# Sparse attention on one core: score products of two heads taken in pairs, the low-key products over 64 rows each

## The reference

```python
def dsa_attention(q, k, v, q_idx, k_idx, w_idx, k_top):
    ...
        rel = jax.nn.relu(jnp.einsum('bqhd,bsd->bqhs', qib, k_idx).astype(jnp.float32))
        score = jnp.einsum('bqhs,bqh->bqs', rel, wb.astype(jnp.float32))
        ...
        _, sel = lax.top_k(score, k_top)
        valid = sel <= qpos[None, :, None]
        kg = gather(k, sel)
        vg = gather(v, sel)
        qg = qb.reshape(bsz, Q_BLOCK, n_kv, grp, hd)
        sc = jnp.einsum('bqkgd,bqjkd->bqkgj', qg, kg).astype(jnp.float32) * scale
        sc = jnp.where(valid[:, :, None, None, :], sc, -jnp.inf)
        p = jax.nn.softmax(sc, axis=-1).astype(v.dtype)
        o = jnp.einsum('bqkgj,bqjkd->bqkgd', p, vg)
```

## Time and profile before

| | us |
|---|---|
| median of 3 runs | 3304.93 (3300.85 to 3305.95) |
| the profiled execution | 3304.05 |
| its span | 3302.3 |
| TensorE matmuls busy | 3109.3 (94%) |
| VectorE busy | 2024.6 (61%) |
| ScalarE busy | 1834.1 (56%) |
| mean granted clock of TensorE | 0.975 of full speed |

### The profile page before, as it was taken

How to read it: one execution, slowest core, us unless ns; L and a number is a source line. 1 busy time by engine, 2 the same in 40 slices (tenths; PEclk the granted TensorE clock), 3 DMA queues, 4 the chain that set the end, 5 groups by cost and what they waited for, 6 DMA issues and landing times. The chain is left out here.

```text
span 3302.3 us, 51762 instructions
## 1 busy us (share of the span) xinstructions
PE 3109.3 (94%) x17304; PEld 2649.1 (80%) x17304; DVE 2024.6 (61%) x4677; ACT 1834.1 (56%) x3869; POOL 845.9 (26%) x1363
## 2 busy tenths in 40 slices
PE   7999969999989999999699998999999999979998
PEld 5888858888868877777578777999888888779997
DVE  5767667888845666565689897434356666641112
ACT  6565547777756666665578775211256666632211
POOL 6444411122112121233322112110134444311110
PEclk9999979999999999999899999999999999989999
DMA  4666673536252222223531103444442222243342
GB/s 177 203 200 202 193 162 72 118 73 134 69 195 86 73 81 69 82 88 91 134 90 44 32 20 132 148 153 153 141 136 68 64 75 65 69 156 124 109 128 77
DMA packets 307191, 370.48 MB, mean 112 GB/s; under 512 B 24800, under 2 KB 251936, under 8 KB 303088
## 3 DMA queue, kind: packets, MB, share of 16 engines
q1 hardware_dynamic: 293728, 320.77, 33.4%
q0 software_dynamic: 13200, 46.42, 4.4%
HBM read 216.32 MB, written 150.80 MB: 111 GB/s over the span
## 5 line engine op out<-in xcount | busy, mean ns | idle before, releaser
L93 PE MATMUL i_p_g<-i_hT_lo,i_wh 128*128 128x512 f32 x768 | 308.6, 402 | 8.0 <-DVE i_wl L1710 8.0
L94 PE MATMUL i_p_g<-i_hT_hi,i_wl 128*128 128x512 f32 x768 | 306.3, 399 | 0.0
L95 PE MATMUL i_p_g<-i_hT_hi,i_wh 128*128 128x512 f32 x768 | 306.0, 398 | 0.0
L1728 DVE SCALAR_TENSOR_TENSOR i_score<-i_relu,i_w,i_score 128x1024 f32<-128x1024 f32 (+7 forms) x154 | 155.2, 1024 | 168.7 <-ACT i_relu L1613 166.8
L1623 ACT ACTIVATE i_above<-i_score,i_less 128x2048 bf16<-128x2048 f32 (+13 forms) x140 | 183.1, 1308 | 104.1 <-POOL i_less L1680 67.8
L1121 DVE TENSOR_TENSOR mla_tl<-mla_p_t,mla_th 128x512 fp32r<-128x512 f32 (+1 forms) x320 | 194.2, 609 | 67.6 <-ACT mla_th L1166 61.7
L1166 ACT ACTIVATE mla_th<-mla_p_t 128x512 fp32r<-128x512 f32 (+1 forms) x320 | 168.0, 528 | 89.7 <-PE mla_p_t L1073 87.6
L1121 DVE TENSOR_TENSOR dsa_tl<-dsa_p_t,dsa_th 128x512 fp32r<-128x512 f32 x272 | 186.9, 689 | 48.1 <-ACT dsa_th L1166 44.3
L1158 ACT ACTIVATE dsa_probs<-dsa_probs,dsa_shift 128x640 f32<-128x640 f32 (+7 forms) x192 | 172.1, 896 | 41.0 <-POOL dsa_shift L1190 39.7
L1158 ACT ACTIVATE mla_probs<-mla_probs,mla_shift 128x640 f32<-128x640 f32 (+4 forms) x192 | 171.9, 895 | 26.3 <-POOL mla_shift L1190 22.3
L1613 ACT ACTIVATE i_relu<-i_p_s 128x1024 f32<-128x1024 f32 (+7 forms) x176 | 141.4, 812 | 78.0 <-DVE i_score L1725 39.3
(11 more groups left out here) (349 smaller groups left out, 9860.7 us busy)
## 6 DMA issues: line engine op xcount, KB each, us to landing
scratch_gates<-i_ob SPq DMA_DIRECT2D x95, 256.0 KB, 2.4
m_m<-scratch_gates SPq DMA_DIRECT2D x64, 256.0 KB, 3.9
f_hs<-scratch_h2T SPq DMA_DIRECT2D x16, 1024.0 KB, 9.5
scratch_qkT<-b_th SPq DMA_DIRECT2D x64, 192.0 KB, 2.6
scratch_qkT<-b_tl SPq DMA_DIRECT2D x64, 192.0 KB, 3.0
i_ws<-in_w_in SPq DMA_DIRECT2D x24, 512.0 KB, 4.5
b_xt<-in_x SPq DMA_DIRECT2D x16, 512.0 KB, 4.8
scratch_h<-b_xh POOLq DMA_DIRECT2D x16, 512.0 KB, 3.0
```

Of the source, the lines that this page charges most:

```text
L93: pe.matmul(out, l[0], r[1], start=start, stop=False)
L94: pe.matmul(out, l[1], r[0], start=False, stop=False)
L95: return pe.matmul(out, l[0], r[0], start=False, stop=stop)
L1728: nc.vector.scalar_tensor_tensor(out=acc, in0=r, scalar=w[:, t, h:h + 1], in1=acc, op0=ALU.mult, op1=ALU.add).then_inc(summed, 1)
```

## The change

The score pieces of heads 0 and 1, and of heads 2 and 3, are taken together. TensorE does the high-key product of the even head, that of the odd head, then the low-key product of the even head and that of the odd one. The low-key products no longer run over all 128 rows: the even head's takes the 64 rows of the lower half and the odd head's the 64 rows of the upper half. So that those rows hold the high part of the queries in both, the odd heads' queries lie with their high part in the upper half, and the queries of a block come by four transfers. The product of the queries' low part with the keys' low part is left out. The mla stage keeps its order (paired is False there).

In the diff, score_pieces makes the groups, schedule places a group at once, and the score step on TensorE issues the products:

```diff
+def score_pieces(n, keys, paired):
+    piece = lambda s, c: ("S", n, s, c, c * GT, min(GT, keys[s] - c * GT), (c + 1) * GT >= keys[s])
+    chunks = [-(-k // GT) for k in keys]
+    if paired:
+        return [[piece(s, c), piece(s + 1, c)] for s in (0, 2) for c in range(chunks[s])]
+    return [[piece(s, c)] for s in range(4) for c in range(chunks[s])]
...
-        mine = [("S", n, s, c, k0, min(GT, keys - k0), k0 + GT >= keys)
-                for s, keys in enumerate(u["keys"]) for c, k0 in enumerate(range(0, keys, GT))]
+        mine = score_pieces(n, u["keys"], paired)
         end = max(first[n] - trail, begin)
-        for x, step in enumerate(mine):
-            covered = covers[n][step[2]]
-            free = read[covered[0], last_place(units[covered[0]], covered[1])] if covered else 0
-            at = max(at, free, begin + (x + 1) * (end - begin) // len(mine))
+        for x, group in enumerate(mine):
+            for step in group:
+                covered = covers[n][step[2]]
+                free = read[covered[0], last_place(units[covered[0]], covered[1])] if covered else 0
+                at = max(at, free)
+            at = max(at, begin + (x + 1) * (end - begin) // len(mine))
             assert at <= first[n]
-            pieces.append((at, step))
+            pieces.extend((at, step) for step in group)
...
-                    layer.scores(p_s[:, i % A, 0:w], n, s, k0, w).then_inc(scored, 1)
+                    out = p_s[:, i % A, 0:w]
                     i += 1
+                    if not layer.paired:
+                        layer.scores(out, n, s, k0, w).then_inc(scored, 1)
+                        continue
+                    layer.high_scores(out, n, s, k0, w)
+                    if s % 2 == 0:
+                        even = out
+                        continue
+                    layer.low_scores(even, n, s - 1, k0, w).then_inc(scored, 1)
+                    layer.low_scores(out, n, s, k0, w).then_inc(scored, 1)
...
         for half in range(2):
-            sp.dma_start(self.q[half * HD:(half + 1) * HD, t % 2].bitcast(F32),
-                         self.qbT[half].rearrange("j (r d) t -> d (j r) t", d=HD)[:, :, at])\
-                .then_inc(self.q_in[t % 2], 16)
+            src = self.qbT[half].rearrange("j (r d) t -> r d j t", d=HD)[:, :, :, at]
+            for r in range(2):
+                rows = (half + r) % 2 * HD
+                sp.dma_start(self.q[rows:rows + HD, t % 2, r:H:2].bitcast(F32),
+                             src[r]).then_inc(self.q_in[t % 2], 16)
...
+    def low_scores(self, out, n, s, k0, w):
+        t, g = n // KV, n % KV
+        rows = slice(s % 2 * HD, s % 2 * HD + HD)
+        return self.nc.tensor.matmul(out, self.q[rows, t % 2, 4 * g + s], self.k_lo[rows, g, k0:k0 + w],
+                                     start=False, stop=True)
```

More of the change, by code:

```diff
@@ L844 @@
     exp_width = 2 * GT
+    paired = False
     def pe_start(self, pe): ...
@@ L894, in exp_pieces, with schedule @@
     return [(0, half), (half, keys - half)]
-def schedule(units, covers, trail, output_late, exp_width):
+def score_pieces(n, keys, paired):
[4 more added lines that the diff above has]
+    return [[piece(s, c)] for s in range(4) for c in range(chunks[s])]
+def schedule(units, covers, trail, output_late, exp_width, paired):
     ticks, first, read = [], [], {}
@@ L959, in stage_attention @@
     places, covers = probs_places(units, layer.rooms)
-    steps = schedule(units, covers, layer.trail, layer.output_late, layer.exp_width)
+    steps = schedule(units, covers, layer.trail, layer.output_late, layer.exp_width, layer.paired)
     exps = [step[1:] for step in steps if step[0] == "E"]
@@ L1800 @@
     rooms = (4 * T, 5 * T)
+    paired = True
     def __init__(self, nc, qbT, kbT, vb, mask, oT, early, late):
@@ L1858, in wait_scores @@
         t = n // KV
-        pe.wait_ge(self.q_in[t % 2], 32 * (t // 2 + 1))
+        pe.wait_ge(self.q_in[t % 2], 64 * (t // 2 + 1))
         if n in (0, 4 * KV):
@@ L1897, in wait_bias, with high_scores @@
         dve.wait_ge(self.m_in[n // KV % 2], 16 * (n // KV // 2 + 1))
-    def scores(self, out, n, s, k0, w):
+    def high_scores(self, out, n, s, k0, w):
         t, g = n // KV, n % KV
-        q = self.q[:, t % 2, 4 * g + s]
-        self.nc.tensor.matmul(out, q, self.k_hi[:, g, k0:k0 + w], start=True, stop=False)
-        return self.nc.tensor.matmul(out, q, self.k_lo[:, g, k0:k0 + w], start=False, stop=True)
+        self.nc.tensor.matmul(out, self.q[:, t % 2, 4 * g + s], self.k_hi[:, g, k0:k0 + w], start=True, stop=False)
+    def low_scores(self, out, n, s, k0, w):
[3 more added lines that the diff above has]
+                                     start=False, stop=True)
     def bias(self, n, s, k0, w):
```

## The result

| | before | after |
|---|---|---|
| median of 4 runs, us | 3304.22 (3300.85 to 3305.95) | 3382.19 (3379.43 to 3383.20) |
| ratio | 1 | 1.0234 [1.0218, 1.0249] |
| span of the profiled execution, us | 3302.3 | 3381.4 |
| TensorE matmuls busy | 3109.3 | 3155.5 |
| VectorE, ScalarE busy | 2024.6, 1834.1 | 2027.1, 1842.5 |

The account below looks back on a forecast made before the run. TensorE's own order of work was taken to bound the sparse-attention stage, with VectorE near. Row changes 51, overlap -22, exp waits 30, waits given back -9 and queries 1 summed to +51 us: 3355 us, range 3298 to 3388.

Parts of the forecast that it names:

- The changes of rows, +51 at 0.16 each: TensorE, sparse-attention stage: 320 changes between 128 and 64 rows cost 0.16 us each, 51 us; bounds 35 and 80.
- rival 1: Sparse-attention stage: changes of rows are free and low products overlap; +7, 3312 us; chance 0.22.
- The overlap, -22: TensorE, pairs: second low product runs beside the first in the other half, saving 22 us, between 14 and 30.
- The waits for exps at new units, +30: Units 16 to 31: first transposes wait for the last exp, 30 us together, 24 to 36; unit 31 waits 4.6.
- Given back: Sparse-attention stage: a slower TensorE no longer waits for VectorE, returning 9 of 7.8 and 5.1 us, between 5 and 13.
- the sign that the prediction named, fewer waits for VectorE: TensorE in the sparse-attention stage: fewer waits for VectorE, expected as evidence for the forecast; no separate size.
- nothing else: Late next after the exps: only VectorE's lower halves and with them the value products, three blocks behind; no size.
- The clock: After unit 31's wait TensorE may run at 1.2 GHz for some 3 us; in the range, not the sum.
- Queries, +1: Four query transfers in place of two: 1 us more where TensorE waited for queries once, 3.6 us.
- Rival 2: Sparse-attention stage: nothing overlaps and nothing drains, only the order counts; +34 less some waits, 3337 us; chance 0.10.
- Rival 3: Faster: free changes, full 30 us saved, exps less in the way; -18, 3287 us with 20 of waits; chance 0.13.

Follow-up runs that it names:

- run 2: Kernel before, in its own order, with each low-key product over the 64 rows of its head's half (640 changes of rows): 3392.91 us, ratio 1.0274.
- Run 3: Changed kernel with all low-key products in the lower 64 rows, so that two can't run side by side: 3401.45 us, ratio 1.0291.
- run 9: Changed kernel with score pieces 7 ticks ahead in place of 4 and exps at most every second tick unless late: 3351.66 us, ratio 1.0148.
- run 10: Changed kernel with low-key products over all 128 rows, score pieces 7 ticks ahead and exps at most every second tick unless late: 3328.30 us, ratio 1.0071.
- run 1: Changed kernel with both low-key products over all 128 rows, keeping the paired order and four query transfers: 3371.18 us, ratio 1.0201.
- Run 8: Changed kernel with a unit's score pieces finished 6 ticks before its first block in place of 4: 3362.69 us, ratio 1.0182.
- Runs 5 and 6: 128-row products, high then low per piece, with two pieces placed together: of two heads 3366.86 us, of one head 3315.36 us.
- run 4: Kernel before with only the four query transfers and their layout: 3304.22 us, ratio 1.0000.

## Why the prediction came out as it did

The number was 3355 with a range of 3298 to 3388; the kernel took 3382, slower as forecast and within the range, near its top. The sum was +51 and the time +78, and its terms were off in both directions.

- **The changes of rows, +51 at 0.16 each**: right. The row of the pair has 0.18 (0.09 ahead of the low load, 0.27 from there to the value product), run 2 has 0.14 to 0.17. That it is a price at all, the question on which rival 1 stood, is settled by run 2. (The paragraph on the Trainium skill names the second rival as the one with changes at 0; the first has them at 0 too.) TensorEngine Tiling (Array Packing), Key Properties, in the Trainium skill says that a change of tiling mode drains the engine; the trace agrees with that and adds the size., 96 rows and 128, said nothing about 64 rows.
- **The overlap, -22**: mis-sized. The two low loads and products run beside each other in full, so -30, the upper bound; the assumption that a load can't start before the matmul ahead does, from the earlier trace rows, doesn't hold for loads into different halves. Run 3 shows the step that it saves. The Trainium skill, TensorE: Matmul & The Clock Gate, Part 3, has products in different row groups start 4 ns apart; the records here agree as far as both products take one step.
- **These two together, +29**: by the rows 58 - 30 = +28 when TensorE is the bound, 23 by run 9 less run 10. In the changed kernel they add only 11 to run 1, for its waits are 10 shorter.
- **The waits for exps at new units, +30**: the mechanism was right, the size under: 22.1 us, so +20, and 4.15 at the last unit where 4.6 was worked out. Run 8 takes them away by placing the exps earlier.
- **"Given back", -9: this is the step that failed.** It left 3.9 of the 12.9 us. It said that where TensorE is slower, it no longer waits for VectorE. That holds in run 2, where the waits are gone. It doesn't hold with the order changed: waits for VectorE at score banks and transposes are 28.4 and not 12.9, and 37.0 in run 1; the sign that the prediction named, fewer waits for VectorE, didn't come. The step looked at how busy VectorE is and not at what stands ahead of the score pass in its queue. I had followed ScalarE's burst of exps to the next unit's first transposes, and wrote "nothing else" of what is late next; the copies between the exps were late as well, and their differences, and the score banks behind those. Runs 5 and 6 show that the source is two heads that end together, 63 us against 11 with two pieces of one. Runs 8 and 9 show that it works through the exps: 19.5 us come back when the pieces, and the exps behind them, are two ticks earlier, and 11 more with the exps apart and a third tick. That the burst acts by way of copies, differences and score passes is read from the traces (run 1's place, the longest waits for copies); no run holds up one link by itself.
- **The clock**, left out of the sum: it costs up to 22 us and belonged in it, since the prediction had counted sixteen waits of 1.4 to 4.6 us and the earlier trace rows shows what one of 3.6 leaves behind.
- **Queries, +1**: nothing, run 4; the wait for them fell from 3.6 to 1.8 us.

Put together, the order of steps was forecast at +22 (30 - 9 + 1) and costs +67 in run 1. Rival 2, order alone with no overlap and no price of a change, is that run: 34 less waits was its sum, and it failed by the same step. Rival 3 needed waits at new units under 31 us and got them, 22; the changes of rows and the waits at score banks ate all of it. That the total landed in the range owes something to chance: the order came out 45 above its forecast, and the rest 18 below (29 forecast, 11 measured), as part of it falls into waits that the order makes anyway.

## What to carry to other kernels

A regrouping on the engine that bounds also regroups what the others have to do: write down, for each in-order queue, what now stands ahead of the instruction that the bound engine waits for, and not only how busy that queue is. Here 31 of the 78 us came back with the same products in the same pairs, 19.5 by placing the score pieces two ticks earlier and 11 more with the exps spread. A product over half of the array's rows pays only when two run beside each other and the changes of rows around them cost less than the step saved: with one pair between two changes, 0.36 us stands against 0.23. By the same figures two pairs in a row would save 0.46 for 0.36, which no run tried, and they would put more pieces in one place.

## What was not expected of the hardware

- Two loads into different halves of the array take 0.19 us together, as one alone, although loads over 128 rows follow each other by 0.11 and two into one half take 0.29 (run 3); their two 512-column products take one step of 0.23 (0.50 recorded against 0.73 in one half).
- Changing between 128 and 64 rows costs 0.18 us at full clock in the pair's rows, 0.14 to 0.17 over 640 changes.
- A wait of TensorE of 2.57 or 4.15 us in the stage was followed by matmuls at the 1.2 GHz level (granted clock 0.53 over the 6 us behind the latter). Between 1850 and 2000 us of run 9 the level fell after waits no longer than 1.66 us: that one ends at 1901.61, and from 1904 to 1908 us the clock was 0.50. In the changed kernel a wait of 1.67 us that ends at 1903.77 left it at 1.00. Run 2, in which TensorE didn't wait from 1700 to 2000 us, held 1.00.
